# Own PSUM banks for a second block of tokens, block 0 first, one-word counts, and loop heads at the start of a fetch block

## The chip, the cores and the metric

The kernel runs on one core of one Trainium2 chip. The metric is the device time of one execution in microseconds (us). PE is the tensor engine, ACT the scalar engine, DVE the vector engine, POOL the GpSimd engine, SP the engine that issues the weight loads. Each engine has a sequencer that reads its instructions in order, waits on semaphores, takes branches, and hands the work on.

## The reference

One layer of a decoder trunk for 512 tokens of 1024 channels, float32. A token-mixing half (sliding-window attention and differential attention, merged by gates) comes first and isn't touched. The second half is a mixture of 32 experts, top 4 of 32 for each token:

```python
logits = ht @ w_router + b_router
top_val, top_idx = lax.top_k(logits, 4); top_w = softmax(top_val)
# token slots grouped by expert, each group padded to blocks of 128 rows
gu = xb @ w_gate_up[e] + b_gate_up[e]            # 1024 -> 2048
h  = clamped_swiglu(gu)                          # 1024
ys = (h @ w_down[e] + b_down[e]) * weight        # 1024 -> 1024, summed per token
```

The 2048 token slots fall on 32 experts, 64 on average. An expert with up to 128 tokens has one block of 128 rows, one with more has two to four. How many is known only at run time, from the router. With the inputs used here 35 blocks are worked on.

## The kernel before

**Weights.** An expert has 12 MB of weights, loaded in 12 halves of 1 MB (`gate_up_half`, 8, and `down_half`, 4) into eight slots `rawm`. A product has to be exact to more than one pass of fp32r gives, so each weight half w is split: ACT rounds it to `wh` (`split_high`, L1100, four buffers), DVE subtracts, `wl = w - wh` (`split_low`, L1178, in place). The activations are split in the same way. A half is then 4 x 3 products of 128 x 512 on PE: wh with high, wl with high, wh with low (`multiply`, L1009 to L1011). The first of two halves has a bias product in front (`biased`, L1015).

**An expert.** `xy[b]` holds the gathered rows of block b. PE transposes them, 8 times 128 x 128, into PSUM banks 5 and 6 (`tokens_transposed`, L987); ACT copies the rounded part to `xh` (L1107), DVE the rest to `xl` (L1185). Eight gate and up halves follow. Gate sums are read by ACT (L1117), up sums by DVE (L1208, L1212). The activations `actv` are transposed into banks 5 and 6 too (`act_transposed`, L1001), and copied to `ah` (ACT, L1125) and `al` (DVE, L1193). Four down halves follow, whose sums ACT copies to `xy` (`outputs`, L1140), and POOL scatters them to the rows `y_d` (`scatter`, L1286 and L1289). For the expert two later POOL gathers new rows into the same `xy` (`gather`, L1267 and L1270).

**Order.** `passes` writes out the order. Body e does: the eight gate and up halves of expert e, the token transposes of e + 1, the four down halves of e - 1, the activation transposes of e. Bodies 1 to 30 stand in a hardware loop of 15 passes with two bodies each, one such loop on each of PE, ACT, DVE and SP (POOL has its own); body 0 and body 31 stand outside. Each loop starts with a branch prefetch hint for its closing branch (`hint_back_edge=True`).

**Further blocks.** Code for blocks 1 to 3 stands in front of that for block 0 in every step, under `If(more >= b)` (`Expert.further`, L893). For an expert with one block PE branches over it (L894). On PE this skipped code is three quarters of the loop. `Expert.__init__` reads one word per expert from the table `nk` (L866): 4 times the number of further blocks of all earlier experts, plus the expert's own number. It is taken apart with `// NB` and `% NB`.

**Banks.** Block 0 sums gate in bank 0 and up in bank 1 (down: 0 and 1). Block b > 0 sums both in bank 1 + b, one after the other: `ps[:, 1 + b if b else up, :]`. So up has to wait until gate was read, and one output half for the other. All transposes use banks 5 and 6: the transposes of a second block wait until the first ones were copied by ACT and DVE, and block 1 goes before block 0.

**On ACT and DVE** the copies of the transposed activations of expert e (`act_high`, `act_low`) stand in body e + 1: those of further blocks at its start, those of block 0 behind its first `split`.

## Time and profile before

| | us |
|---|---|
| median of 3 runs (1966.46 to 1977.33) | 1967.62 |
| the profiled execution | 1976.37 |
| its span, first to last instruction | 1974.6 |
| PE busy | 1702.7 |
| DVE busy | 1315.6 |
| ACT busy | 1028.1 |
| POOL busy | 250.7 |
| mean granted clock of PE | 0.925 |

The span has three parts: up to about 500 us the token-mixing half and the router, from there to about 1917 us the experts, then the weighted sum of the experts' rows. Matmul durations overlap in the records: a product of 128 x 512 is shown with 0.39 us and the next starts 0.23 us after it. So starts are compared, and idle time, not the sum of durations. The clock is shown as a share of 2.4 GHz; 0.50 is 1.2 GHz. A row with `q` behind the engine's name is one of its sequencer.

### The profile page before, as it was taken

The page shows a single profiled execution, that of the slowest core. Times are in us where ns is not written, and L with a number is a line of the kernel's source. Part 1 is how long each engine was busy: PE and PEld are TensorE (multiplying, and loading weights), DVE is VectorE, ACT ScalarE, POOL GpSimd, SP SyncE. Part 2 cuts the span into 40 slices and gives each one's busy share as a digit, 9 for nine tenths or more (in the row PEclk, how much of TensorE's full clock was granted, in tenths as well). Part 3 has the DMA queues.
Part 4 walks back from the last instruction along what each step waited for, and adds up shares of the span by engine and source line. Part 5 has one row for each costly group of instructions (what it writes and reads, how often), then busy time and mean ns, then how long its engine had stood idle before and what let it go on. Part 6 is the DMA issues. An engine that isn't in the chain of part 4 may idle for free.

```text
span 1974.6 us, 24769 instructions
## 1 busy us (share of the span) xinstructions
PE 1702.7 (86%) x7526; PEld 1314.8 (67%) x7527; DVE 1315.6 (67%) x1024; ACT 1028.1 (52%) x922; POOL 250.7 (13%) x232
## 2 busy tenths in 40 slices
PE   6999976695389998899999999898999998989860
PEld 1688854443368777777777877776777786767650
DVE  0454468734378887466888888855688888456645
ACT  2323234421357776355777777644567776445530
POOL 2000000112201111001111111110111111101110
PEclk8899986787589999999999999998999999989985
DMA  7575430011689998566999999955799999567835
GB/s 228 199 243 204 149 120 1 25 57 53 227 292 362 351 364 300 203 246 245 344 357 354 361 345 362 359 207 207 251 353 355 355 358 340 197 213 254 300 138 220
DMA packets 245566, 498.54 MB, mean 252 GB/s; under 512 B 16811, under 2 KB 17927, under 8 KB 244737
## 3 DMA queue, kind: packets, MB, share of 16 engines
q1 hardware_dynamic: 228288, 458.26, 64.9%
q0 software_dynamic: 14448, 34.72, 5.2%
q8 instruction: 201, 3.29, 0.7%
q10 hardware_dynamic: 2610, 2.11, 0.3%
q14 instruction: 19, 0.16, 0.0%
HBM read 490.22 MB, written 27.09 MB: 262 GB/s over the span
## 4 chain that ended last, share of the span: by engine, by line
PE 66%; issue 4%; DMA 4%; DVE 3%; ACT 2%; POOL 1%; DVEq 1%; ACTq 0%; POOLq 0%
PE ps L1009 19%; PE ps L1011 19%; PE ps L1010 19%; PE ps L621 3%; PE ps L1015 3%; PE ps L987 2%; DMA xy<-h_ffn,icur 1%; PE ps L1001 1%; DMA expert_rows<-xy,icur 1%; DMA x1e<-x_after_mixing 1%; ACT wh L1100 1%; POOL icur L1286 1%; PE ps L641 0%; DVE wl L1178 0%; DVE yo L1343 0%
## 5 line engine op out<-in xcount | busy, mean ns | idle before, releaser
L1178 DVE TENSOR_TENSOR wl<-rawm,wh 128x2048 fp32r<-128x2048 f32 x384 | 876.1, 2290 | 323.6 <-ACT wh L1100 318.0
L1100 ACT ACTIVATE wh<-rawm 128x2048 fp32r<-128x2048 f32 x384 | 736.2, 1918 | 484.0 <-PE ps L1011 480.3
L1009 PE MATMUL ps<-wh,xh 128*128 128x512 f32 x1120 | 473.6, 423 | 1.4 <-issue 1.1
L1011 PE MATMUL ps<-wh,xl 128*128 128x512 f32 x1120 | 442.5, 395 | 1.9 <-issue 1.7
L1010 PE MATMUL ps<-wl,xh 128*128 128x512 f32 x1120 | 442.9, 395 | 0.0
L1009 PEld LDWEIGHTS ps<-wh,xh 128*128 128x128 f32 x1120 | 216.2, 193 | 48.5 <-issue 8.2
L1011 PEld LDWEIGHTS ps<-wh,xl 128*128 128x128 f32 x1120 | 214.2, 191 | 47.0
L1010 PEld LDWEIGHTS ps<-wl,xh 128*128 128x128 f32 x1120 | 215.4, 192 | 44.4
L1009 PE MATMUL ps<-wh,ah 128*128 128x512 f32 x560 | 236.0, 421 | 0.0
L1010 PE MATMUL ps<-wl,ah 128*128 128x512 f32 x560 | 221.6, 396 | 0.0
L1011 PE MATMUL ps<-wh,al 128*128 128x512 f32 x560 | 221.4, 395 | 0.0
L1286 POOL COPY icur<-stab 128x1 int32 (+1 forms) x35 | 53.0, 1514 | 982.0 <-ACT xy L1140 982.0
L1011 PEld LDWEIGHTS ps<-wh,al 128*128 128x128 f32 x560 | 107.1, 191 | 23.3
L1010 PEld LDWEIGHTS ps<-wl,ah 128*128 128x128 f32 x560 | 107.4, 192 | 22.4
L1015 PE MATMUL ps<-bparts,sel 96*128 96x512 bf16 x210 | 84.1, 401 | 44.2 <-ACT actv L1117 14.9
L1009 PEld LDWEIGHTS ps<-wh,ah 128*128 128x128 f32 x560 | 108.3, 193 | 20.9
L1666 DVE TENSOR_TENSOR wlf<-raw,whf 128x2048 fp32r<-128x2048 f32 (+1 forms) x18 | 39.1, 2174 | 100.7 <-ACT whf L1442 100.7
L987 PE MATMUL ps<-ident,xy 128*128 128x128 f32 x280 | 40.1, 290 | 46.6 <-DMA xy<-h_ffn,icur 30.3
L1015 PEld LDWEIGHTS ps<-bparts,sel 96*128 (+1 forms) x210 | 20.6, 98 | 88.6 <-issue 57.6
L1270 POOL DMA_INDIRECT xy<-h_ffn,icur x35 | 67.5, 1930 | 31.8 <-POOL icur L1267 28.3
L1545 PE MATMUL ps<-whf,hh 128*128 128x512 f32 (+1 forms) x192 | 71.4, 372 | 0.0
L1547 PE MATMUL ps<-whf,hl 128*128 128x512 f32 (+1 forms) x192 | 71.1, 370 | 0.0
(224 smaller groups left out, 1692.4 us busy)
## 6 DMA issues: line engine op xcount, KB each, us to landing
rawm<-in_w_gate_up SPq DMA_DIRECT2D x256, 1024.0 KB, 6.5
rawm<-in_w_down SPq DMA_DIRECT2D x128, 1024.0 KB, 6.5
raw<-in_w_ada SPq DMA_DIRECT2D x24, 1024.0 KB, 10.0
raw<-in_w_in SPq DMA_DIRECT2D x16, 1024.0 KB, 5.4
yt<-expert_rows POOLq DMA_DIRECT2D x4, 2048.0 KB, 9.4
wo<-in_w_out SPq DMA_DIRECT2D x2, 2048.0 KB, 17.9
bias_vectors_repeated<-bias_vectors POOLq DMA_DIRECT2D x1, 2304.0 KB, 16.1
xs<-in_x ACTq DMA_DIRECT2D x1, 2048.0 KB, 25.4
```

The lines of the kernel that those rows point to most:

```text
L621: ins = nc.tensor.matmul(ps[:, 2 * b + half, :], src[:, k, t * P:(t + 1) * P], wo[:, 4 * b + k, half * UN:(half + 1) * UN], start=(k == 0) ...
L987: ins = nc.tensor.transpose(ps[:, 5 + k // 4, (k % 4) * P:(k % 4 + 1) * P], xy[b][:, k * P:(k + 1) * P], ident[:])
L1009: nc.tensor.matmul(dst, a_h[:, b, kk, :], wh[:, place.split(v), k, :], start=False, stop=False)
L1010: nc.tensor.matmul(dst, a_h[:, b, kk, :], wl[:, place.slot(v), k, :], start=False, stop=False)
L1011: ins = nc.tensor.matmul(dst, a_l[:, b, kk, :], wh[:, place.split(v), k, :], start=False, stop=kk == KC - 1)
L1015: nc.tensor.matmul(dst, sel[:, bass.ds(e, 1)].to_broadcast([96, P]), bias, start=True, stop=False)
L1100: nc.scalar.activation(flat(wh[:, place.split(v), :, :]), flat(rawm[:, place.slot(v), :, :]), ACT.Copy).then_inc(wh_done, 1)
L1178: nc.vector.tensor_tensor(flat(wl[:, place.slot(v), :, :]), flat(rawm[:, place.slot(v), :, :]), flat(wh[:, place.split(v), :, :]), ALU.sub ...
L1270: pool.indirect_dma_start(out=xy[b][:], out_offset=None, in_=h2_d, in_offset=bass.IndirectOffsetOnAxis(ap=icur[:, 0, b:b + 1], axis=0), bo ...
L1286: nc.gpsimd.tensor_copy(icur[:, 1, b:b + 1], stab[:, b, bass.ds(x.e + 1, 1)]).then_inc(scur[m], 1)
L1545: nc.tensor.matmul(dst, a_h, b_h, start=first, stop=False)
L1547: return nc.tensor.matmul(dst, a_l, b_h, start=False, stop=last)
```

## The change

Five edits go together.

1. **Banks.** A table `summed(b, n)` gives block 1 banks 2 (gate, first output half) and 7 (up, second output half); blocks 2 and 3 have one bank each, 3 and 4. `turned(b)` gives odd blocks banks 3 and 4 for their transposes, even ones 5 and 6.
2. **Order of blocks.** Both transposes and their copies on ACT and DVE do block 0 first, then the further ones (`first_then_further`). Since banks 3 and 4 belong to two uses, PE has new waits in the branches for further blocks, all on counts of earlier experts.
3. **act_high and act_low** as a whole move to the end of body e.
4. **Counts.** `nk` has two words per expert: the expert's own number, and the sum over earlier ones (`prefix`). The first is read in `__init__`; the second only in the branches for further blocks, once in each. The product that makes the table has 68 columns instead of 34.
5. **Heads.** The loops of PE, ACT, DVE and SP get `head_slot={eng.engine: 0}`: their first instruction is placed at the first place of a fetch block.

```diff
-    pick = NB * np.triu(np.ones((E, E + 2), np.float32), 2) + np.eye(E, E + 2, 1, dtype=np.float32)
+    pick = np.concatenate([np.eye(E, E + 2, 1, dtype=np.float32), np.triu(np.ones((E, E + 2), np.float32), 2)], 1)
...
-        nc.vector.tensor_copy(nk[:], ps[0:1, 5, 0:E + 2]).then_inc(nk_ready, 1)
+        nc.vector.tensor_copy(nk[:], ps[0:1, 5, 0:2 * (E + 2)]).then_inc(nk_ready, 1)
...
+    def turned(b):
+        return ps[:, 3:5, :] if b % 2 else ps[:, 5:7, :]
+    def summed(b, n):
+        return ps[:, ((0, 1), (2, 7), (3, 3), (4, 4))[b][n], :]
...
-            both = eng.value_load(nk[0:1, bass.ds(e + 1, 1)], min_val=0, max_val=NB * (T * TOPK // P) + NB - 1)
-            self.before = eng.snap(both // NB)
-            self.more = eng.snap(both % NB)
+            self.more = eng.value_load(nk[0:1, bass.ds(e + 1, 1)], min_val=0, max_val=NB - 1)
+        def prefix(self):
+            self.before = self.eng.value_load(nk[0:1, bass.ds(self.e + (E + 3), 1)], min_val=0, max_val=T * TOPK // P)
+            return self.before
...
+        def first_then_further(self, work, rest=None):
+            work(0)
+            self.further(work, rest)
+        def further(self, work, rest=None):
             with self.eng.If(self.more >= 1):
+                self.prefix()
                 work(1)
                 for b in range(2, NB):
                     with self.eng.If(self.more >= b):
                         work(b)
+                if rest is not None:
+                    rest()
...
-        with nc.Fori(0, E // 2 - 1, engines=[eng.engine], hint_back_edge=True) as k:
+        with nc.Fori(0, E // 2 - 1, engines=[eng.engine], hint_back_edge=True, head_slot={eng.engine: 0}) as k:
...
# tokens_transposed
             def work(b):
-                m = min(b, 1)
-                if b:
-                    pe.wait_ge(xg_in[1], (x.before + x.more) * 16)
-                    pe.wait_ge(xl_done[1], x.count(1, 0, b) - 1)
+                if b == 0:
+                    pe.wait_ge(xg_in[0], (e + 1) * 16)
                 else:
-                    pe.wait_ge(xg_in[0], (e + 1) * 16)
-                    pe.wait_ge(xl_done[1], x.all_more(1, 0))
+                    if b == 1 and not begins:
+                        acts = Expert(pe, e - 1).prefix() + START
+                        if not (isinstance(e, int) and e == 1):
+                            outputs = Expert(pe, e - 2).prefix() * U_D + START
+                        pe.wait_ge(al_done[1], acts)
+                        if not (isinstance(e, int) and e == 1):
+                            pe.wait_ge(y_copied[1], outputs)
+                        pe.wait_ge(g_ready[1], x.earlier(T_GU, 1))
+                        pe.wait_ge(u_ready[1], x.earlier(T_GU, 1))
+                    if b == 1:
+                        pe.wait_ge(xg_in[1], (x.before + x.more) * 16)
...
# act_transposed
+                if b == 1:
+                    tokens = x.before + x.more if last else Expert(pe, x.e + 2).prefix()
+                pe.wait_ge(act_ready[min(b, 1)], x.count(T_GU, 1, b))
+                if b == 1:
+                    pe.wait_ge(xl_done[1], tokens + START)
+                    pe.wait_ge(y_copied[1], x.before * U_D + START)
...
# gate_up_half_used
-                dst = ps[:, 1 + b if b else up, :]
+                dst = summed(b, up)
+                if v == 0 and b:
+                    outputs = Expert(pe, x.e - 1).prefix() * U_D + START if has_d else None
+                    pe.wait_ge(xl_done[1], x.all_more(1, 0))
+                    if has_d:
+                        pe.wait_ge(y_copied[1], outputs)
+                        pe.wait_ge(al_done[1], x.earlier(1, 1))
+                        pe.wait_ge(u_ready[1], x.earlier(T_GU, 1))
...
# down_half_used
-                    elif t:
+                    elif b > 1 and t:
                         pe.wait_ge(y_copied[1], x.count(U_D, 0, b))
...
# body of ACT; DVE's in the same way with act_low
-            if has_d:
-                act_high(before, before.further)
             for v in range(N_GU + N_D if has_d else N_GU):
                 split_high(place, v + SPL)
-                if v == 0 and has_d:
-                    act_high(before, at_once)
...
+            act_high(x)
```

## Rows read from the trace of the kernel before

**Rows 1.** The page, engines: busy us, share of the span, instructions.

```profile
PE 1702.7 (86%) x7526; PEld 1314.8 (67%) x7527; DVE 1315.6 (67%) x1024; ACT 1028.1 (52%) x922; POOL 250.7 (13%) x232
```

**Rows 2.** The page, chain of waits by line: share of the span.

```profile
PE ps L1009 19%; PE ps L1011 19%; PE ps L1010 19%; PE ps L621 3%; PE ps L1015 3%; PE ps L987 2%; DMA xy<-h_ffn,icur 1%; PE ps L1001 1%; DMA expert_rows<-xy,icur 1%; DMA x1e<-x_after_mixing 1%; ACT wh L1100 1%; POOL icur L1286 1%; PE ps L641 0%; DVE wl L1178 0%; DVE yo L1343 0%
```

**Rows 3.** Windows: us, busy of PE, PEld, DVE, ACT, POOL, clock, DMA share, GB/s.

```profile
1031.96:1067.88 35.92, 35.92 (x167) 29.14 (x166) 31.91 (x19) 26.68 (x18) 5.13 (x4) 1.00 1.00 365
1067.88:1105.00 37.12, 36.44 (x167) 29.02 (x166) 31.91 (x19) 26.79 (x18) 5.96 (x4) 1.00 0.98 351
```

**Rows 4.** Windows, three stretches with a second block, eight plain experts.

```profile
771.81:947.18 175.37, 154.86 (x675) 123.87 (x673) 105.44 (x64) 85.86 (x61) 18.53 (x14) 0.94 0.67 237
1275.20:1448.63 173.43, 152.36 (x674) 121.83 (x673) 105.40 (x64) 85.90 (x61) 19.08 (x14) 0.95 0.68 242
1667.89:1841.90 174.01, 151.74 (x674) 121.45 (x673) 105.37 (x64) 85.88 (x61) 18.80 (x14) 0.95 0.67 239
958.54:1251.55 293.01, 289.63 (x1330) 232.65 (x1329) 255.26 (x145) 213.86 (x144) 43.64 (x32) 1.00 0.99 357
```

**Rows 5.** Waits of PE (us, times, longest), then one row of its timeline.

```profile
PE ps L987 <- DMA xy<-h_ffn,icur: 30.3, 4, 21.8
PE ps L987 <- DVE xl L1185: 16.2, 3, 5.4
PE ps L1015 <- ACT actv L1117: 14.9, 6, 2.5
PE ps L1001 <- DVE al L1193: 13.9, 3, 4.7
PE ps L1015 <- ACT xy L1140: 7.5, 3, 2.5
...
778.25 1.97 PE L987 MATMUL ps<-ident,xy 128*128 128x128 f32 x8 [5.41 <-DVE xl L1185]
```

**Rows 6.** Windows, two stretches at the lower clock.

```profile
777.42:784.25 6.83, 6.00 (x18) 5.02 (x19) 2.00 (x2) 1.02 (x1) 0.00 (x0) 0.50 0.18 64
808.14:811.55 3.41, 3.24 (x8) 2.58 (x9) 1.95 (x1) 0.60 (x2) 0.00 (x0) 0.50 0.77 298
```

**Rows 7.** Line 1270, the gathers at 757.3 and 760.8, and their landing.

```profile
L1270 POOL DMA_INDIRECT xy<-h_ffn,icur x2: 1047/1644/2242, 757.3 to 760.8; - x2
DMA to landing us min/median/max: 8.8/8.8/8.8
```

**Rows 8.** Lines 866 and 925, 1134 to 1142: ns min/median/max, first and last start.

```profile
L866 PEldq TENSOR_LOAD <-nk x2: 308/308/308, 1140.0 to 1140.8; - x2
L925 PEldq COMPARE_BRANCH  x1: 960/960/960, 1138.8 to 1138.8; - x1
```

**Rows 9.** Timeline of PE at the same head.

```profile
1140.92 1.04 PE L1001 MATMUL ps<-ident,actv 128*128 128x128 f32 x8
1142.32 0.39 PE L1015 MATMUL ps<-bparts,sel 96*128 96x512 bf16 x1 [0.37 <-issue]
```

**Rows 10.** Timeline of ACT and of DVE behind a body's end.

```profile
1109.03 1.92 ACT L1100 ACTIVATE wh<-rawm 128x2048 fp32r<-128x2048 f32 x1 [1.43 <-PE ps L1011]
1110.86 1.01 ACT L1125 ACTIVATE ah<-ps 128x1024 fp32r<-128x1024 f32 x1
1110.98 2.29 DVE L1178 TENSOR_TENSOR wl<-rawm,wh 128x2048 fp32r<-128x2048 f32 x1 [1.54 <-ACT wh L1100]
```

**Rows 11.** DMA queues, 1066 to 1139.7: packets, MB, share of the time.

```profile
q8 instruction: 12, 0.20, 1.1%
```

**Rows 12.** Line 894, 1131.2 to 1134.9, and 1854 to 1860: ns and starts.

```profile
L894 PEldq COMPARE_BRANCH  x2: 225/294/364, 1131.3 to 1134.2; - x2
...
L894 PEldq COMPARE_BRANCH  x2: 236/2529/4822, 1854.5 to 1859.6; - x2
```

**Rows 13.** Timeline of PE at the loop's exit.

```profile
1859.50 0.58 PE L1015 MATMUL ps<-bparts,sel 96*128 96x512 bf16 x1 [3.58 <-issue]
...
1883.86 0.39 PE L1015 MATMUL ps<-bparts,sel 96*128 96x512 bf16 x1
```

More of the change, by code:

```diff
@@ L851, in program @@
     y_half_copied = [sem("y_half_copied0"), y_copied[0]]
[L853 removed]
+    passed = sem("passed")
     START = 1
@@ L1050, in work @@
             def work(b):
-                dst = ps[:, 1 + b if b else t, :]
-                if d == 0:
-                    pe.wait_ge(al_done[min(b, 1)], x.all_more(1, 0) if b else x.count(1, 0, 0))
+                dst = summed(b, t)
+                if d == 0 and b == 0:
+                    pe.wait_ge(al_done[0], x.count(1, 0, 0))
+                if d == 0 and b:
+                    gate_ups = x.before + x.more if after is None else x.before + x.more + after.more
+                    if b == 2:
+                        tokens = gate_ups if after is None or is_last(after.e) else Expert(pe, after.e + 2).prefix()
+                        pe.wait_ge(xl_done[1], tokens + START)
+                    pe.wait_ge(al_done[1], x.all_more(1, 0))
+                    pe.wait_ge(y_copied[1], x.earlier(U_D, 1))
+                    pe.wait_ge(u_ready[1], gate_ups * T_GU + START)
                 if h == 0:
@@ L1106, in work @@
                 act.wait_ge(xt_done[m], x.count(1, 0, b))
-                nc.scalar.activation(flat(xh[:, b, :, :]), flat(ps[:, 5:7, :]), ACT.Copy).then_inc(xh_done[m], 1)
-            x.blocks(work)
+                nc.scalar.activation(flat(xh[:, b, :, :]), flat(turned(b)), ACT.Copy).then_inc(xh_done[m], 1)
+            x.first_then_further(work)
         def gate(x, t, place, v):
@@ L1134, in work @@
                     if after is not None:
-                        act.wait_ge(xt_done[1], after.all_more(1, 0))
+                        act.wait_ge(xt_done[1], x.before + x.more + after.more + START)
                     act.wait_ge(y_out[1], x.stored(1))
@@ L1167, in body @@
                     outputs(before, v // 2 - 4, place, v, after)
+            act_high(x)
         passes(act, body)
         end = Expert(act, E - 1)
-        act_high(end, end.blocks)
         outputs(end, 0, LAST, 1, None)
@@ L1225, in body @@
             before = Expert(dve, e - 1) if has_d else None
-            if has_d:
-                act_low(before, before.further)
             for v in range(N_GU + N_D if has_d else N_GU):
@@ L1233, in body @@
                 split_low(place, v + SPL)
-                if v == 0 and has_d:
-                    act_low(before, at_once)
             if not has_d:
                 tokens_low(Expert(dve, e + 1))
+            act_low(x)
         passes(dve, body)
-        end = Expert(dve, E - 1)
-        act_low(end, end.blocks)
     def experts_pool(pool):
```

138 lines of the change are left out of this document (72 added, 66 removed).

## The prediction

> **What bounds the kernel now.** The page first. PE is busy 86% of the span, DVE and ACT 67% and 52% [rows 1]; in the chain that ended last the product lines (L1009 to L1011) alone hold 57% [rows 2]. So I read PE and ask when it doesn't run at its own pace. An expert in the middle of the loop is 144 products and 16 transposes, from 1031.96 to 1067.88: 35.92 us, PE busy throughout at clock 1.00 [rows 3]. Neither wait nor weight sets that length; its DMA share is 1.00 at 365 GB/s, so the loads have little room either. Three kinds of time are lost around it.
>
> First, the experts that have a second block: 35 gathers for 32 experts, so there are three, and one trip from their token transposes until the third expert after takes 175.37, 173.43 and 174.01 us [rows 4]. Its work is four periods of 35.92 (three experts, and the second block's 144 products) and 0.9 for the transposes at its end: 144.6. 89.1 us are lost over the three, with the clock at 0.94 and 0.95. The waits of PE [rows 5] name them: 16.2 and 13.9 us in front of the second transposes of tokens and activations (they need banks 5 and 6 back, by DVE xl and al), 14.9 in front of a bias product while gate and up share the block's one bank (ACT actv), 7.5 the same for the two output halves (ACT xy), 8.5 of the 30.3 on the gather (21.8 is the first expert's). Some of these are followed by stretches at the lower clock level, 1.2 GHz: 6.83 us of 0.50 after the 5.41 wait [rows 6].
>
> Second, the loop head. An expert that begins a pass takes 37.12 instead of 35.92 [rows 3]. Over the eight periods from 958.54 to 1251.55 (293.01 us [rows 4]), with four heads in them, it is 5.65 us over 8 x 35.92: 1.41 a head. I count 14 back edges; those after a slow stretch cost near nothing, in sum about 14.5 us.
>
> Third, what the change leaves: attention, routing, the first gather, the tail.
>
> **The change, part by part.** *Own banks.* A second block's gate and up get banks 2 and 7, so the 14.9 and the 7.5 go. Its transposes go to 3 and 4 and no longer wait for 5 and 6: the 16.2 and 13.9 go. With them goes most of the slow clock. What is late next? ACT and DVE have twice the time per half there, so not they. Scatter and gather stay: the gather that lets the third expert after begin is issued by POOL behind two scatters and the second's landing, none of which moves. Its 8.5 us stay, bounds 0 and 9.
>
> *What the new code adds.* A prefix is now read apart, and `Expert(pe, e - 1).prefix()` reads both words. One read is 0.78 us from one load to the next [rows 8]. In front of the second block's token transposes stand five reads, 3.9 us, and a few waits on counts that were reached an expert ago, 0.6. PE's queue covers about 3.2: PE's sequencer has issued the activation transposes when the closing branch starts, at 1138.8, and they end at 1141.96 [rows 8, 9]. That leaves a gap of 1.3 to 1.6 and perhaps 0.8 of slow clock, 3 x 2.4 = 7.2; at the first gate half three reads more, 0.8 for the expert that starts mid-pass. Bounds: 0 if all is covered, 3 x 4.5 + 3.4 = 17 if nothing is.
> Of the 89.1, 8.5 (gather), 1.5 (the head in the third stretch), 8.0 (reads) and 1 for ends stay: **-70**, bounds -80 and -55.
>
> *First transposes lead.* PE does block 0 first. The gathers still go second block first; block 0's, issued at 760.8, landed 8.8 us later for transposes at 771.81 [rows 4, 7]: 2 us of room, so nothing.
>
> *act_high and act_low move to the end of the body.* On ACT it will follow the last output copy, before the next weight rounding. Idle ahead of that is 1.43 us, and ah takes 1.01; on DVE the idle is 1.54 and al takes some 1.22 [rows 10]. Both fit: nothing. Without the cover it would be 0.2 us a period at a queue four halves deep, still nothing on PE. DVE's `rest` and ACT's waits concern the three experts alone.
>
> *One-word counts.* At a head PE's sequencer reads two experts, divides and takes remainders; now one read and no arithmetic, -0.9 us, of which at most the visible 0.4 to 0.5 gap counts. In the others it is under the queue. POOL's chain gets 0.8 shorter at best. The wider count product and copy, once, are below 0.1.
>
> *Aligned heads.* Here the sign is decided. PE's loop body is 2878 instructions (counted in the compiled program of before), of 64 B. In the 73 us of a pass 12 instruction packets of 0.20 MB in all arrive [rows 11]: 16 KB, 256 instructions each, so the body is fetched anew in every pass. Where in a block does it lie? The branches over a further block take 222 to 250 ns, but some 340 to 464: those that jump into another block (one of each in rows 12). They fit one placing only: head at place 114, closing branch at place 175 of the twelfth block. And the branch that enters that block, at 1134.2, takes 364 ns [rows 12]; the closing branch, issued at 1138.8, is through 960 ns later [rows 8], 5.5 us after the entry. The other passes show the same 5.3 to 5.5; where PE was slow it takes only 353. So the loop's first block is asked for when the last is entered, and is there some 5.4 us later. Where a block wasn't asked for at all, at the loop's exit, the branch stands 4822 ns, and PE has a gap of 3.58 us and slower products behind it [rows 12, 13].
> The change makes the body longer: 14 skipped prefix reads per expert at 4 instructions each (56), and on balance 21 more for reads and waits in the first gate half, 18 for tokens, 16 for the first output half, 10 for activations, less 2: 119, and 117 for the pass's other expert, 3114 in all. With the head at place 0 the closing branch is at place 41 of a thirteenth block (29 to 53 with my counting error). And the activation transposes now come first, with some 70 skipped instructions between them and the branch. So the last block is entered by that skip, and the closing branch is reached at once: it will stand 5 us in every pass instead of 0.7 to 1.5. From the skip: 5.4 to the head, 1.65 to the first product (2.55 now, from 1139.8, 0.2 ahead of the first read, to 1142.32, less one read and the arithmetic [rows 8, 9]), less 3.2 of queue: PE idle 3.9, where it is 0.4 to 0.5 now. The nearest row is the exit: idle 3.58, then 24.4 for 96 products that take 22.75 at full clock (1.6 of slow clock) [rows 13]. I take 4.0 + 1.5 = 5.5 a head, bounds 0 (found in time) and 7.4 (the slow clock lasts 6.83 as after the 5.41 wait). The second stall, when the block after the head's is late too, goes, as a head at place 0 has a whole block to run on; it is inside the 1.41.
> 14 x 5.5 = 77, and 2.7 more at each of the two heads where a second block is due, less 14.5 now: **+68**. The exit now runs on within its block: 5.4 becomes 2, -3.5. Entry: one branch, +1. And behind a late head the gather of 8.5 is no longer late in two of three cases, -5.7. Heads in all: +60.
> ACT's body has 252 instructions, DVE's 253, and no instruction packets are theirs in the loop; 50 more leave that so: 0, bounds 0 and 30.
>
> The Trainium skill ("Runtime: NRT & Kernel Launch", Instruction fetch mechanics) has blocks of 16 KiB with 256 instructions, as the packets here show, and says that the next page is fetched while the current one runs, so that a crossing is "mostly hidden". By that rule heads cost nothing, and the sum is the first rival's. The rows speak for a fetch that is hidden only where 5.4 us of work are left in the block.
>
> **Sum.** -70 + 60 = -10, against the profiled execution, 1976.4 (span 1974.6 and 1.8 around it), which lies 8.8 above the median of 1967.6; I go by the median: **1957**.
>
> **Rivals.**
> *The closing branch finds its block.* My count is off by over 41, or the loop's first block is asked for earlier than I read. Then the 14.5 of the heads fall to about 1 instead: -70 - 13 + 1 = -82: 1886 (if the heads only stay as they are, 1898). For it: I have counted code that I haven't seen compiled. Against: 41 of 236 is much, and the 5.4 us recur in each pass.
> *The heads outweigh the banks.* One mechanism, the closing branch: 4.0 us idle and after it the long half-clock stretch, 3.4 lost, at every head. 14 x 7.4 + 5.4 - 14.5 - 3.5 + 1 - 5.7 = +86; less 70: +16, 1984. It decides from (70 + 5.7 + 14.5 + 2.5 - 5.4)/14 = 6.2 us a head. For it: 6.83 us at 0.50 after a 5.41 us wait; against: 3.41 us after a 2.49 one (808.14 on), and 1.6 lost after the 3.58 one [rows 5, 6, 13].
> *The banks don't do it.* PE waits for the reads instead and half of the 70 is lost: -35 + 60 = +25: 1992. Against: the reads are priced by their rows and small.
>
> **How the numbers follow.** Forecast 0.58 (its own range 1935 to 1977), block found in time 0.28, heads outweigh 0.11, banks fail 0.03. 0.5%, what a measurement of this kernel tells, is 10 us: within the forecast, at -10, 0.31 is faster, 0.24 same, 0.03 slower. With the 0.28 faster and 0.14 slower: 0.59, 0.24, 0.17. Range 1884 to 1984.
>
> **What would show it.** The closing branch (L925, PE's sequencer) at about 5000 ns in 14 passes, and a gap of 4 us in front of each odd expert's first bias product, followed by a clock of 0.50; 13 instruction packets a pass. Token and activation transposes of a second block without a wait on xl or al, no wait on actv or xy. The prediction is wrong if the closing branch stands below 1 us: then the time is near 1886.

## The result and the profile after

The changed kernel takes **1978.97 us** (median of 20 runs, 1971.69 to 1985.96), the kernel before beside it 1972.16 us (20 runs, 1964.47 to 1980.11): a ratio of 1.0035, 95% interval 1.0022 to 1.0047. It is slower by some 7 us, a third of a per cent; the forecast, 1957, lies 10 us under the kernel before by its own sum.

The page of the changed kernel, engines and the queue of instruction blocks (columns as in [rows 1] and [rows 11]):

```profile
span 1979.5 us, 24740 instructions
PE 1707.8 (86%) x7526; PEld 1321.7 (67%) x7527; DVE 1317.6 (67%) x1024; ACT 1030.1 (52%) x922; POOL 226.7 (11%) x232
q8 instruction: 217, 3.56, 0.7%
```

PE is busy for as long as before [rows 1]; 217 blocks of instructions arrive, where the kernel before had 201. The waits of PE, us in total, times, longest, to be held against [rows 5]:

```profile
PE ps L1057 <- issue: 54.0, 16, 6.4
PE ps L993 <- DMA xy<-h_ffn,icur: 27.0, 2, 21.7
PE ps L1057 <- DVE wl L1225: 21.4, 6, 5.6
PE ps L993 <- issue: 5.8, 3, 2.6
```

The 52.5 us on DVE xl, DVE al, ACT actv and ACT xy in the three stretches are gone. In their place stand 54.0 us in front of bias products (L1057), for which no releaser is found: the instruction came late. 49.5 us of them stand at ten of the 14 loop heads. Of the six put down to DVE wl four lie at heads too (3.65, 3.93, 3.84, 3.60 us): at the second of them wl was written by 1070.4 and the sequencer past its first skip by 1070.6, so there the two end almost together, and run 4 below, where neither is left, tells which of them leads. The next rows say by what: the closing branch (L943) over the whole run, then around one head the skip over the activation transposes of further blocks (L909) and the closing branch (ns min/median/max, first and last start), and the gap that PE shows there:

```profile
L943 PEldq COMPARE_BRANCH  x16: 89/4819/5876, 557.0 to 1862.2; - x16
...
L909 PEldq COMPARE_BRANCH  x1: 995/995/995, 1142.1 to 1142.1; - x1
L943 PEldq COMPARE_BRANCH  x1: 5739/5739/5739, 1143.3 to 1143.3; - x1
...
1144.39 1.04 PE L993 MATMUL ps<-ident,actv 128*128 128x128 f32 x8
1150.73 0.60 PE L1057 MATMUL ps<-bparts,sel 96*128 96x512 bf16 x1 [5.30 <-issue]
```

The skip enters the last block at 1143.1, the closing branch is through at 1149.0: 5.9 us. The instruction packets (queue q8) have times of their own. The head's block starts to move at 1146.5 here; at another head the last block was entered at 909.8 and the packet starts at 911.1, where the DMA engines were less busy. The q8 row of the windows 1146.50:1146.62 and 911.04:911.14, the closing branch of that second head, and both fetches as windows (columns as in [rows 3]):

```profile
q8 instruction: 1, 0.02, 56.3%
q8 instruction: 1, 0.02, 67.1%
L943 PEldq COMPARE_BRANCH  x1: 3547/3547/3547, 910.0 to 910.0; - x1
909.81:913.52 3.71, 2.92 (x17) 2.27 (x16) 0.88 (x1) 1.63 (x1) 0.00 (x0) 1.00 0.41 137
1143.13:1149.03 5.90, 2.30 (x15) 1.77 (x13) 4.78 (x3) 3.97 (x4) 1.50 (x1) 0.91 1.01 373
```

At all 14 heads the packet takes 0.9 to 1.1 us and the closing branch is through 1.36 to 1.54 us after its end. So the branch stands for this block and for nothing else; what differs is the time from the entry of the last block to the packet's start, 1.3 to 3.6 us (6.0 where the last block was entered early).

Windows of the changed kernel (columns as in [rows 3]): a head's expert, a plain one, another head's, the half-clock stretch behind its gap, one whole pass, and the three stretches of [rows 4]:

```profile
1065.95:1108.47 42.52, 38.59 (x167) 30.88 (x166) 31.99 (x19) 26.78 (x18) 3.74 (x4) 0.92 0.86 308
1108.47:1144.39 35.92, 35.92 (x167) 29.14 (x166) 31.99 (x19) 26.80 (x18) 5.59 (x4) 1.00 1.01 359
1144.39:1187.67 43.28, 37.98 (x168) 30.44 (x167) 32.01 (x19) 26.77 (x18) 3.74 (x4) 0.92 0.84 301
1147.94:1154.77 6.83, 4.04 (x10) 3.18 (x11) 2.03 (x2) 0.00 (x0) 2.63 (x4) 0.50 0.33 122
1065.95:1144.39 78.44, 74.51 (x333) 60.03 (x332) 63.98 (x37) 53.58 (x36) 9.33 (x8) 0.96 0.93 331
777.91:940.54 162.63, 150.25 (x674) 120.40 (x673) 102.33 (x61) 84.91 (x61) 16.19 (x14) 0.96 0.72 250
1288.80:1451.73 162.93, 151.02 (x674) 120.93 (x673) 102.34 (x61) 84.89 (x61) 16.39 (x14) 0.96 0.72 252
1687.79:1850.76 162.97, 148.71 (x674) 119.41 (x673) 106.74 (x64) 86.11 (x61) 18.54 (x14) 0.97 0.72 256
```

A head costs 42.52 - 35.92 = 6.6 and 43.28 - 35.92 = 7.4 us here, where it was 1.2 [rows 3]. The three stretches fell from 522.8 to 488.5 us. That gain and those heads cancel.

### The profile page after: what moved, and what is told of

It reads as the page before. It is cut to its first block, busy times and chain, and to the rows that moved or that the text cites. A ratio compares the mean times of both kernels' runs of the same rounds, so it can differ in the third digit from the quotient of the medians.

```text
span 1979.5 us, 24740 instructions
## 1 busy us (share of the span) xinstructions
PE 1707.8 (86%) x7526; PEld 1321.7 (67%) x7527; DVE 1317.6 (67%) x1024; ACT 1030.1 (52%) x922; POOL 226.7 (11%) x232
## 4 chain that ended last, share of the span: by engine, by line
PE 68%; DVE 4%; issue 4%; DMA 2%; ACT 2%; POOL 1%; POOLq 0%; ACTq 0%; DVEq 0%
PE ps L1051 20%; PE ps L1053 19%; PE ps L1052 19%; PE ps L621 3%; PE ps L1057 3%; PE ps L993 2%; DVE wl L1225 2%; ACT wh L1154 2%; DMA x1e<-x_after_mixing 1%; DMA xy<-h_ffn,icur 1%; DMA expert_rows<-xy,icur 1%; PE ps L641 0%; DVE yo L1388 0%; PE ps L634 0%; ACT h2t L692 0%
## 5 line engine op out<-in xcount | busy, mean ns | idle before, releaser
L1051 PE MATMUL ps<-wh,xh 128*128 128x512 f32 x1120 | 479.3, 428 | 0.0
L1052 PE MATMUL ps<-wl,xh 128*128 128x512 f32 x1120 | 448.0, 400 | 0.0
L1053 PE MATMUL ps<-wh,xl 128*128 128x512 f32 x1120 | 447.6, 400 | 0.2 <-issue 0.2
L1057 PE MATMUL ps<-bparts,sel 96*128 96x512 bf16 x210 | 84.9, 404 | 80.1 <-issue 54.0
L1057 PEld LDWEIGHTS ps<-bparts,sel 96*128 (+1 forms) x210 | 20.5, 98 | 124.4 <-issue 119.4
L1591 PE MATMUL ps<-wlf,hh 128*128 128x512 f32 (+1 forms) x192 | 71.0, 370 | 0.0
## 6 DMA issues: line engine op xcount, KB each, us to landing
bias_vectors_repeated<-bias_vectors POOLq DMA_DIRECT2D x1, 2304.0 KB, 15.7
```

The lines of the kernel that those rows point to most:

```text
L1051: nc.tensor.matmul(dst, a_h[:, b, kk, :], wh[:, place.split(v), k, :], start=False, stop=False)
L1052: nc.tensor.matmul(dst, a_h[:, b, kk, :], wl[:, place.slot(v), k, :], start=False, stop=False)
L1053: ins = nc.tensor.matmul(dst, a_l[:, b, kk, :], wh[:, place.split(v), k, :], start=False, stop=kk == KC - 1)
L1057: nc.tensor.matmul(dst, sel[:, bass.ds(e, 1)].to_broadcast([96, P]), bias, start=True, stop=False)
L1591: nc.tensor.matmul(dst, a_h, b_l, start=False, stop=False)
```

## The experiments

**Theory A**, the prediction's own: PE's closing branch stands until the head's block of 256 instructions is there, 5.4 us from the moment the last block was entered. **Rival B**: the new code itself (reads, waits, a longer body) costs the time, wherever the head lies. The first four runs move the head without touching the work, or the work without the head.

**1. The changed kernel, PE's head at place 110**

```diff
-        with nc.Fori(..., hint_back_edge=True, head_slot={eng.engine: 0}) as k:
+        with nc.Fori(..., hint_back_edge=True,
+                     head_slot={eng.engine: 110 if eng.engine == mybir.EngineType.PE else 0}) as k:
```

> The changed kernel with PE's loop head at place 110 of a block of 256 instructions instead of place 0 (other engines stay). The closing branch then lies at place 143 of the thirteenth block, and that block is entered by the skip behind the output halves, some 12 us of PE work ahead of the branch, as in the kernel before.
> Theory A (the head's block is asked for when the last block is entered, and is there 5.4 us later): the closing branch takes 0.3 to 1.5 us instead of 3.5 to 5.9, the gaps of 2.5 to 6.4 us in front of odd experts' bias products fall below 1 us, the half-clock stretches of 6.83 us behind them go, and the gain of the banks shows alone: 1972 - 70 = about 1902 (1890 to 1915).
> Rival B (the added reads, waits and the longer body cost the time, wherever the head lies): the closing branch still takes over 3 us or the gaps move elsewhere, and the time stays within 10 us of the changed kernel, 1970 to 1985.

Measured: 1951.87 us, ratio 0.9908 [0.9880, 0.9935]. Faster than the changed kernel, so the place counts, but above theory A's 1890 to 1915 and below rival B's 1970 to 1985: 50 us short of A's 1902. One end of a pass, two skips (L909) and the closing branch:

```profile
L909 PEldq COMPARE_BRANCH  x1: 4104/4104/4104, 1043.2 to 1043.2; - x1
L909 PEldq COMPARE_BRANCH  x1: 2787/2787/2787, 1049.2 to 1049.2; - x1
L943 PEldq COMPARE_BRANCH  x1: 3463/3463/3463, 1054.0 to 1054.0; - x1
```

These are three crossings into a new block, each of which stands. The first ends at 1047.3, the second at 1051.9 (4.7 us later), the third at 1057.5 (5.5 later). It isn't the closing branch alone: any crossing waits that comes too soon behind the one before.

**2. The changed kernel, heads not placed** (`head_slot` left away: head at about place 160)

> The changed kernel with no placing of the loop heads at all: PE's head falls at about place 160 of a block, and its closing branch at about place 193 of the thirteenth, with more than 5.4 us of work in that block.
> Theory A: the closing branch is short (0.3 to 1.5 us), but the first branch of the pass, which jumps over the second block's token transposes from instruction 6 to 120 of the body, now leaves the head's block at once. The next block has been asked for only when the head's was entered, so this branch stands 4 to 5 us instead: the same stall a branch later, and the time is about that of the changed kernel, 1965 to 1985.
> Rival B (only the closing branch's own jump back is dear, a crossing elsewhere is mostly hidden): both are short, time about 1900.
> Rival C (aligning the heads is what saves time): slower than the changed kernel by over 10 us.

Measured: 1963.46 us, 0.9959 [0.9941, 0.9977]. That is 1.5 us below theory A's range, and the stall moved as it has it, from the closing branch to the first skip:

```profile
L943 PEldq COMPARE_BRANCH  x1: 1164/1164/1164, 1053.0 to 1053.0; - x1
...
L909 PEldq COMPARE_BRANCH  x1: 4207/4207/4207, 1055.3 to 1055.3; - x1
```

Aligning the heads cost 15 us against leaving them alone, enough to turn a change of -0.4% into one of +0.35%. But it isn't what took most of the gain, as both layouts lose 6 to 7 us in each quiet pass.

**3. The kernel before, its heads at place 0**

```diff
-        with nc.Fori(0, E // 2 - 1, engines=[eng.engine], hint_back_edge=True) as k:
+        with nc.Fori(0, E // 2 - 1, engines=[eng.engine], hint_back_edge=True, head_slot={eng.engine: 0}) as k:
```

> The kernel before with nothing changed but its loop heads, which are aligned to blocks. PE's body of 2878 instructions then ends at place 61 of the twelfth block, entered by the skip behind the activation transposes of its further blocks; block 0's 16 transposes and a wait stand between that and the branch.
> Theory A: the closing branch takes 3.5 to 5 us in each of 14 passes, PE idles 3 to 5 us in front of the next bias product with half clock behind it, 50 to 75 us in all: 2020 to 2045. The difference between this kernel and the changed one is then the gain of the banks by itself, -50 to -70.
> Rival B (the new code costs the time, not the place of the head): within 10 us of the kernel before, 1962 to 1982.

Measured: 2008.78 us, 1.0191 [1.0164, 1.0217], below the 2020 to 2045 of theory A; closing branch 3882 ns in the median. Rival B falls: with not one instruction of the new code, the aligned head alone costs 38 us. The changed kernel is 30 us faster than this one: less than the -50 to -70 expected for the banks, and its own heads lose more (6.6 to 7.4 us a quiet pass against 3.5 to 6.0 here).

**4. The changed kernel, trimmed by 48 instructions**

```diff
-                self.prefix()
+                if prefix:
+                    self.prefix()
...
-            x.blocks(work)
+            x.blocks(work, prefix=h == 0)     # gate and up halves, output halves
```

The prefix isn't used where it is left away. PE's body is 3058 instructions, the closing branch at place 241 of the twelfth block.

> The changed kernel with its heads aligned as they are, but without the read of the prefix in the second gate, up and output half (h = 1), where nothing uses it. That takes 48 instructions out of PE's body: 3058, so that the closing branch falls at place 241 of the twelfth block, which is entered by a skip behind an output half, over 5.4 us of work ahead; 12 blocks a pass instead of 13.
> Theory A: no stall at the closing branch (0.3 to 0.5 us) and none behind the head, whose block is whole: both stalls of a head are gone, and the time is 1972 - 70 - 13 = about 1889 (1878 to 1905). Instruction packets: 12 a pass.
> Rival B (a head at place 0 itself is dear, or the new waits are): the closing branch stays over 3 us, time 1965 to 1985.

Measured: 1914.45 us, 0.9726 [0.9698, 0.9755]. The line of the closing branch, one pass, and the three stretches:

```profile
L944 PEldq COMPARE_BRANCH  x16: 89/452/1144, 555.3 to 1786.4; - x16
...
1038.74:1110.59 71.85, 71.85 (x334) 58.29 (x333) 64.00 (x37) 53.55 (x36) 10.84 (x8) 1.00 1.01 361
760.62:918.33 157.71, 147.81 (x674) 118.80 (x673) 106.72 (x64) 86.10 (x61) 22.60 (x14) 0.98 0.75 267
1242.00:1399.88 157.88, 147.96 (x674) 118.95 (x673) 106.64 (x64) 86.10 (x61) 22.34 (x14) 0.97 0.77 271
1615.69:1776.36 160.67, 149.21 (x675) 119.77 (x673) 106.73 (x64) 86.09 (x61) 20.65 (x14) 0.97 0.75 263
...
PE ps L994 <- DMA xy<-h_ffn,icur: 37.7, 4, 22.0
PE ps L994 <- issue: 7.5, 3, 2.7
...
L909 PEldq COMPARE_BRANCH  x27: 222/227/2845, 1039.2 to 1108.3; - x27
```

Both stalls of a head are gone: the pass is 71.85 us with PE busy in all of it, twice the plain expert's 35.92 [rows 3]. The last row, the skips of the same pass, shows that blocks still come late: five of the 27 skips stand 2.0 to 2.8 us. Each time PE has enough in its queue, and loses nothing. That it is 1914 and not 1878 to 1905 is the stretches' doing: they hold 476.3 us, only 46.6 under [rows 4]: the waits on a gather behind the first expert's are 37.7 - 22.0 = 15.7 us, where they were 8.5 [rows 5].

**A new theory D** was tried next: the number of blocks is what bounds a pass (12 or 13, some 5.95 us each).

**5. The changed kernel without the hint** (`hint_back_edge=True` left away)

> The changed kernel without the hint that names the closing branch to the instruction fetch (hint_back_edge is left away; the heads stay aligned, same instructions otherwise but for the hint itself).
> Theory A (in the changed kernel the closing branch is reached right after the last block is entered, and the hint can only start the fetch of the head's block at that entry): without it the fetch starts at the branch itself, so the branch stands 4.8 us and more instead of 3.5 to 5.9; the pass gets 0 to 1 us longer and the time is 1975 to 1995. At the exit the next block is then the one that was asked for.
> Rival B (the hint is what makes the branch dear, for instance since it displaces the fetch of the next block): the branch is shorter than now by over 1 us, 1960 or less.
> Rival C (the hint still saves much): slower by over 20 us, 2000 or more.

Measured: 2002.92 us, 1.0141 [1.0102, 1.0180]; the branch 6248 ns in the median, up to 7556. That is rival C's (2000 or more, slower by over 20), and theory A misses by 8 us: the hint is worth 1.4 us a pass at the branch even though it comes late, and 24 us in all, where theory A had at most 1 us a pass. Without it 230 blocks arrive instead of 217 (`q8`), one more in most passes. At one closing branch, entered at 1154.8, two packets follow, at 1157.2 and 1158.3: first the block behind the last, in vain, then the head's.

**6. The kernel before, padded to 13 blocks**

```diff
                 for b in range(2, NB):
                     with self.eng.If(self.more >= b):
                         work(b)
+                        if b == 2 and self.eng.engine == mybir.EngineType.PE:
+                            for _ in range(3):
+                                self.eng.value_load(nk[0:1, bass.ds(self.e + 1, 1)], ...)
```

> The kernel before with its own banks, reads and waits, but with code added that never runs: three reads of a count inside each section for a third block (no expert here has one), on PE alone, 252 instructions a pass. PE's body is then 3130 instructions, its head at place 111 and its closing branch at place 168 of the thirteenth block, where the kernel before has 114 and 175 of the twelfth. Only the number of blocks that a pass runs through differs, 13 for 12.
> Theory D (new, from the runs so far: a block is asked for when the one before it is entered and is there 5.4 to 6.0 us later, so that a pass can't be shorter than its number of blocks by some 5.95 us: 71.4 for 12, 77.4 for 13; the passes without a second block took 71.8 us with 12 blocks and no stall at the head, 77 to 78.5 with 13 blocks wherever the head lay): quiet passes of 76.5 to 78.5 us instead of 73.0 to 73.5, branches over skipped sections that stand 1.5 to 4 us, and 14 x 3 to 5 us more: 2012 to 2045.
> Theory A alone (only the place of the closing branch counts): the closing branch stays at 0.7 to 1.5 us and the time within 10 us of the kernel before, 1962 to 1982.

Measured: 1972.19 us, 1.0009 [0.9986, 1.0032]. Theory D falls, 1972 for its 2012 to 2045: 252 instructions and one block more a pass, and nothing lost over the run. Passes of 72.6 and of 75.9 us stand side by side, so it is near an edge:

```profile
q8 instruction: 218, 3.57, 0.7%
...
1063.36:1135.92 72.56, 72.11 (x333) 58.16 (x332) 63.81 (x37) 53.45 (x36) 11.10 (x8) 1.00 1.00 357
1135.92:1211.83 75.91, 73.61 (x333) 59.41 (x332) 63.82 (x37) 53.36 (x36) 10.81 (x8) 0.98 0.96 347
```

**7. The trimmed kernel, PE's head at place 110**

> The run with 3058 instructions in PE's body (no read of the prefix in the second halves) with the head at place 110 instead of 0. The instructions that run are the same; the pass now runs through 13 blocks instead of 12, and the closing branch is at place 95 of the last.
> Theory D (number of blocks by 5.95 us): quiet passes of 76.5 to 78 us instead of 71.8, total 1914 + 14 x 3 to 5 = 1945 to 1985.
> Rival E (the 48 instructions fewer are what saved the time, by themselves): the time stays within 12 us of that run, 1902 to 1926.

Measured: 1967.68 us, 0.9960 [0.9932, 0.9987]; closing branch 4152 ns, quiet passes 76.9 to 78.7 us. Rival E falls: the 48 instructions fewer save nothing by themselves, what counts is where they put the edges. Theory D had the right number here for a wrong reason, as run 6 shows.

What is left, **theory T**: a block is asked for when the one before it is entered, and comes 4.7 to 6 us later (at two heads behind a second block's stretch 3.7); it costs what the block's own work, and the some 3 us that PE still has in its queue, don't cover. Not all of a block is work: a section of a further block is jumped over in 0.22 us and fills a third of one. I added up each layout's pass instruction by instruction (product 0.2365 us, transpose 0.1125, branch 0.24, load of a count 0.35, other register work 0.09, queue 3.2, and 5.4, 5.7 or 6.0 from a block's entry to the next). The sum is an estimate, and its single steps aren't printed here. The next three runs were chosen by that sum.

**8. The trimmed kernel, PE's head at place 16**

> The trimmed kernel (3058 instructions in PE's body) with the head at place 16 instead of 0. That moves every instruction of the loop by 16 places and changes none of them; the closing branch then lies at place 17 of the thirteenth block instead of place 241 of the twelfth, and that block is entered by the skip behind the activation transposes, 1 instruction or two before the branch.
> Theory T (a block is asked for when the block before it is entered and is there 5.4 to 6.0 us later; it costs where less work than that is left in a block, less the some 3 us that PE has in its queue; what counts is where the edges fall in the pass, not their number): closing branch 4 to 6 us, quiet passes of 76.5 to 79 us instead of 71.8 to 72.3, total 1914 + 14 x 4.5 to 7 = 1975 to 2010.
> Rival E (the 48 instructions fewer save the time by themselves): within 12 us of the trimmed kernel, 1902 to 1926.

Measured: 1983.69 us, 1.0065 [1.0042, 1.0089], as theory T has it. The closing branch lies at place 1 of the thirteenth block (241 + 16 = 257), not at 17 as expected; the skip still enters that block right in front of it. Sixteen places, no instruction changed, and 69 us lost against the trimmed kernel. Over the run, then a pass (against the 71.85 of run 4):

```profile
L944 PEldq COMPARE_BRANCH  x16: 89/5176/5937, 557.6 to 1866.2; - x16
...
1070.51:1149.25 78.74, 73.62 (x334) 59.40 (x333) 64.01 (x37) 53.56 (x36) 9.57 (x8) 0.98 0.93 332
```

**9. and 10. The kernel before, PE's head at places 128 and 208**

```diff
-        with nc.Fori(0, E // 2 - 1, engines=[eng.engine], hint_back_edge=True) as k:
+        with nc.Fori(0, E // 2 - 1, engines=[eng.engine], hint_back_edge=True,
+                     head_slot={eng.engine: 128} if eng.engine == mybir.EngineType.PE else None) as k:
```

> The kernel before with its loop head on PE at place 128 of a block instead of 114, nothing else. The last block is then entered by an earlier skip, and the block behind the head is left later.
> Theory T: adding up the pass instruction by instruction, with 5.4 to 6.0 us from entering a block to the next one and 3.2 us of queue, PE idles 0 to 0.9 us a pass instead of 1.2 to 2.7. Closing branch 0.3 to 0.7 us, quiet passes of 71.8 to 72.8 us instead of 73.0 to 73.5, total 1972 - 14 x 0.7 to 1.3 = 1954 to 1963.
> Rival H (the 1.4 us of a head in the kernel before is the branch and the reads themselves, not the fetch): within 4 us of the kernel before.

Measured: 1966.06 us, 0.9974 [0.9953, 0.9996]: 4 us less, not the 9 to 18 expected. The quiet passes kept 72.9 to 73.2 us; the sum is some 1 us a pass too kind to this place. By its time alone this run doesn't tell theory T from rival H. The trace shows where the stall went, to the second skip behind the head (3137 here, 2.3 to 3.4 us in the quiet passes):

```profile
L894 PEldq COMPARE_BRANCH  x2: 231/1684/3137, 1133.9 to 1137.3; - x2
```

The sum hangs on 3 us of queue that I took to be always there; that the queue was short at this skip is my reading, no run varied it.

> The kernel before with its loop head on PE at place 208, nothing else: the same 2878 instructions. The closing branch falls at place 13 of the thirteenth block, entered right ahead of it, and the first skip behind the head, from instruction 11 to 97, crosses into the next block at once, while that one has only been asked for on entering the head's.
> Theory T: two fetches stand one behind the other: closing branch 4.7 to 5.3 us and the first skip 3.6 to 4.2, PE idle 7.5 to 8.7 us a pass instead of 1.2 to 2.7 and slow clock behind it; quiet passes of 79.5 to 83 us, total 1972 + 14 x 6 to 10 = 2056 to 2112.
> Rival B (late code costs once per pass at most): 2020 to 2045, as with the head at place 0.
> Rival E (placing doesn't matter without the new code): within 10 us of the kernel before.

Measured: 2066.43 us, 1.0475 [1.0443, 1.0507], in the range of theory T and out of both rivals'. The closing branch (L925) over the run, PE's first skips (L894) behind one head, and that pass:

```profile
L925 PEldq COMPARE_BRANCH  x16: 88/4738/6177, 558.6 to 1946.9; - x16
L894 PEldq COMPARE_BRANCH  x2: 237/1562/2886, 1102.3 to 1105.8; - x2
...
1061.88:1143.41 81.53, 74.75 (x333) 60.20 (x332) 63.82 (x37) 53.43 (x36) 9.01 (x8) 0.94 0.91 321
```

Two fetches stand one behind the other: 4.7 us at the branch, 2.9 at the first skip. The same 2878 instructions take 100 us more than at place 128.

**11. The trimmed kernel, POOL scatters block 0 first**

```diff
-            x.blocks(work)
+            x.first_then_further(work)      # in scatter()
```

> The trimmed kernel (no read of the prefix in the second halves, head at place 0, 12 blocks a pass), and POOL scatters an expert's block 0 ahead of its second block. The gather that lets the third expert after begin waits for block 0's scatter to land; in the trimmed run that scatter was the second of two (issued at 897.32, landed 905.70, gather issued at 908.32, landed 916.37) and PE waited some 5.3 us for the gather at each of the three places, with 2 us of slow clock behind it.
> Theory F: block 0's scatter is issued first, some 4 us earlier, and the gather with it: the wait of PE on the gather falls from 5.3 to about 1 us or goes, with its slow clock: 3 x 4 to 7 us less, 1914 - 12 to 21 = 1893 to 1902.
> Rival G (the gather waits for the transfers' own rate, or for POOL's second scatter in front of it): within 4 us of the trimmed run, 1910 to 1918.

Measured: 1896.99 us, 0.9607 [0.9572, 0.9642]: 17 us less than run 4, within theory F's 1893 to 1902. Of the waits on the gather for the third expert after, 4.9, 5.5 and 5.4 us in run 4, one of 1.0 is left; two of 1.3 and 1.1 are new, ahead of an expert with a second block. Theory F holds.

**12. The same, and one-word reads of a prefix**

```diff
+    def prefix_of(eng, e):
+        return eng.value_load(nk[0:1, bass.ds(e + (E + 3), 1)], ...)
...
-                        acts = Expert(pe, e - 1).prefix() + START
+                        acts = prefix_of(pe, e - 1) + START
...
-                            outputs = Expert(pe, e - 2).prefix() * U_D + START
+                            outputs = prefix_of(pe, e - 2) * U_D + START
...
-                    tokens = x.before + x.more if last else Expert(pe, x.e + 2).prefix()
+                    tokens = x.before + x.more if last else prefix_of(pe, x.e + 2)
```

> The trimmed kernel with POOL's scatter of block 0 first, and with the reads of an earlier or later expert's prefix reduced to the one word that is used: in front of a second block's token transposes three reads instead of five, ahead of its activation transposes two instead of three. Each read took 0.64 to 0.78 us on PE's sequencer, and PE idled 2.1 us in front of the second token transposes with 3 us of slow clock behind.
> Theory R (the reads are what keeps PE waiting there): 1.3 to 1.5 us less idle before each of three token transposes, and the slow clock behind them gone, 3 x 1.5 to 4.5: 1897 - 5 to 13 = 1884 to 1892.
> Rival S (another wait ends last there): within 3 us of 1897.

Measured: **1889.12 us**, 0.9585 [0.9547, 0.9624], the fastest of all. The medians differ from run 11 by 8 us, the ratios by 4, and their intervals overlap; what decides is PE's idle time before the three second token transposes, 3.2, 3.3 and 3.4 us in run 11 and 1.9, 1.9 and 1.9 here, as theory R has it. The three stretches:

```profile
760.43:911.60 151.17, 146.96 (x675) 118.30 (x674) 102.39 (x61) 84.89 (x61) 16.59 (x14) 0.99 0.75 264
1235.81:1386.04 150.23, 145.36 (x675) 117.07 (x674) 102.46 (x61) 84.88 (x61) 18.66 (x14) 1.00 0.76 270
1601.50:1752.87 151.37, 147.03 (x674) 118.32 (x674) 101.71 (x61) 84.33 (x61) 19.55 (x14) 0.99 0.75 263
```

452.8 us: 70.0 less than [rows 4]. The figure forecast for the banks is there, but not by the forecast's parts: that one still had 8.5 us of gather and 8.0 of reads standing, and here the gather is earlier, the reads are fewer and no late head lies in the stretches.

**All layouts together.** "Sum" is PE's idle time a pass by the added-up pass, at 5.4 and at 6.0 us a block; "over" is what the quiet passes (no second block; those from about 1000 to 1260 us) took beyond 71.84, half clock included.

| run and kernel | PE instructions in the loop's body | head at | closing branch at | it takes, median ns | sum, us | over, us | time, us |
|---|---|---|---|---|---|---|---|
| 4 trimmed | 3058 | 0 | 241 of 12th | 452 | 0 | 0.0 | 1914 |
| 12 fewer reads | 3037 | 0 | 220 of 12th | 460 | 0 | 0.0 | 1889 |
| 9 before | 2878 | 128 | 189 of 12th | 781 | 0 to 0.9 | 1.0 to 1.4 | 1966 |
| before | 2878 | 114 | 175 of 12th | 744 | 1.2 to 2.7 | 1.2 to 1.6 | 1972 |
| 6 padded | 3130 | 111 | 168 of 13th | 980 | 1.2 to 5.7 | 0.7 to 4.1 | 1972 |
| 1 changed | 3106 | 110 | 143 of 13th | 1008 | 1.5 to 5.7 | 4.4 to 7.2 | 1952 |
| 3 before | 2878 | 0 | 61 of 12th | 3882 | 3.6 to 4.5 | 3.5 to 6.0 | 2009 |
| 7 trimmed | 3058 | 110 | 95 of 13th | 4152 | 3.8 to 6.2 | 5.1 to 6.9 | 1968 |
| changed | 3106 | 0 | 33 of 13th | 4819 | 3.8 to 5.7 | 6.6 to 7.4 | 1979 |
| 8 trimmed | 3058 | 16 | 1 of 13th | 5176 | 3.8 to 5.7 | 6.7 to 6.9 | 1984 |
| 2 changed | 3106 | 160 | 193 of 13th | 784 | 4.3 to 5.8 | 6.5 to 6.7 | 1963 |
| 10 before | 2878 | 208 | 13 of 13th | 4738 | 7.5 to 8.7 | 9.7 to 10.2 | 2066 |

The sum was made after runs 1 to 7; runs 8 to 10 are its test, and run 9 its miss. It leaves out the half clock, which I take to be most of what "over" has beyond it. The places are worked out from the head's place and the count.

## Why the prediction was wrong

The mechanism was right: the banks' waits went, and late heads took the gain back. The sign came out wrong since **three terms were mis-sized**, all to the good side. By the prediction's own steps, on the profiled executions (spans of 1974.6 and 1979.5). Its base was low too: 1967.6 from three runs, where twenty give 1972.16, so the same -10 would read 1962.

- *Own banks, -89.1 of waits.* Right: no wait on xl, al, actv or xy is left in the three stretches. No engine behind them became the bound.
- *What the new code adds, 8.0.* Too small. PE idles 2.0, 2.6 and 1.1 us before the second token transposes, 0.8 to 1.0 before the bias products behind them, 0.7 to 0.8 at the first gate half of the expert that starts in mid-pass, some 1.7 at a head in front of the second block's, and slow clock follows most of them: in all some 19, against 8 and the 1 for ends. The reads behind the tokens' were taken as covered by the queue; as I read it, the queue is still short from the first gap when they come. Run 12 makes three reads less in each of the three places and gets 8 us back. **+10.**
- *The gather is no longer late in two of three cases, and its 8.5 stay at most.* It was hidden at two places, but the third wait is 5.3 us with some 3 of slow products behind it, as much as the three cost before. So nothing of the -5.7 came. With the heads mended it gets worse, 15.7 us (run 4): the experts ahead of it got faster, POOL's chain didn't. **+6.**
- *Aligned heads, 14 x 5.5.* The step that failed most plainly in its bounds: my 1.5 us of slow clock behind the gap was taken from the exit [rows 13], where the gap was 3.58. The gaps are 2.5 to 6.4 us, 4.6 in the mean (sum of 14: 64.5; I had 4.0), and around ten of them the clock stands at 0.50 for 6.83 us, as [rows 6] showed around the 5.41 gap, around the other four for 3.41. The length doesn't follow the gap: one of 3.93 has the long stretch, one of 5.31 the short. By what the transposes and the first products of each head take beyond their own pace it is some 92 us over 14 heads, 6.6 a head (4.2 to 8.5, so past my upper bound of 7.4), where 77 + 5.4 were forecast. The rival "the heads outweigh the banks" decided from 6.2 us a head and gave 1984; it is what happened, though with smaller heads than its 7.4 and with the reads' and the gather's help, so that its 1984 comes so near is partly luck. **+9.**
- *Why 4.6 and not 4.0.* I started the 5.4 us at the skip; in five passes the last block itself wasn't there when the skip wanted it (995 to 1089 ns, 368 to 466 in eight others). The chain of late blocks begins before the head.
- *Exit, -3.5.* Right, and a little more: 89 ns for the branch, no gap where 3.58 stood; some -6 with its slow products. *ACT's and DVE's bodies, act_high and act_low, the wider count product*: nothing seen, as forecast. *First transposes lead*: the first ones waited for nothing.
- The count of PE's body was 3114; it is 3106, the closing branch at place 33 for the forecast 41. *"The closing branch finds its block"* at 0.28 was too much for that: its condition was a miscount by over 41. Its time, 1886, is that of run 12 within 3 us, but that run is had by 69 instructions less and a shorter chain on POOL.

-10 + 10 + 6 + 9 is +15, less 2 to 3 more at the exit and some 5 by which the two profiled executions differ ahead of the first expert's products (the first gather is issued at 517.4 before and 513.0 after), which no part of the change explains: +7, with +5 between the two spans and +7 between the medians.

A block that is crossed "mostly hidden", the rule of the Trainium skill ("Runtime: NRT & Kernel Launch", Instruction fetch mechanics) that the prediction weighed, is borne out for PE's time by the passes of run 4 (12 crossings, nothing lost, though the sequencer stood up to 2.8 us) and not by those of the changed kernel (6.6 to 7.4 us a pass). The same section warns that a taken branch out of the two pages at hand stalls for its fetch; the closing branch of run 5, which has no hint and takes 6248 ns, is that case. The first skip of run 2 stood 4.2 us though it only jumps into the next block.

**Still open.** Why a block takes 4.7 us from entry to entry at one place and 5.9 at another. In the changed kernel it is 3.7 at the two heads where the DMA engines are less than half busy (0.41 at the one shown), and 4.3 to 6.0 at the 11 where they are 0.98 busy and more, so the packet may wait behind the weight loads. But in run 3 two heads at 0.56 and 0.62 took 5.3 and 5.4 like the rest, and no run varied the loads: it isn't shown. Open too are why place 128 gave only 4 us, and what the banks alone are worth with both heads silent and the old reads, which wasn't run (runs 4 and 9 stand 52 us apart, with 1.0 to 1.4 us of head a pass in the latter).

## What to carry to other kernels

This loop's body of some 3000 instructions was streamed anew in every pass, one block ahead. For a body like it, count what work PE has between one block edge and the next, skipped code included: sixteen places can move an edge onto a branch and cost 70 us (runs 4 and 8), and the same edit can look good or bad by where it puts the edges. Judge a change of code inside such a loop only with the head placed for each version. And when a wait is taken away, look for the chain that runs beside it (here POOL's scatters and gather): it gets back part of the gain unless it is shortened as well.

## What the runs showed of the hardware that I had not expected

- The same 2878 instructions take 1966 us with the loop head at place 128 of a block and 2066 at place 208; 3058 take 1914 at place 0 and 1984 at place 16.
- Not only the closing branch stalls: a skip behind the head stood 4.2 us (run 2), a skip inside the output halves 4.1 (run 1).
- The hint for the back edge still saves 24 us when the last block is entered right in front of the closing branch (run 5), and 13 blocks more arrive without it.
- A branch that jumps over a section within its block takes mostly 215 to 237 ns, into a block that is there 420 to 470, and 338 to 372 when it is the first jump behind an edge that was crossed in line, without leaving the block. I had read the last kind as a crossing in [rows 12]. That these are the three kinds is inferred from where the edges lie.
- From the end of a block's packet to the end of the branch that waited for it are 1.36 to 1.54 us at all 14 heads of the changed kernel; the packet itself takes 0.9 to 1.1.
- 252 instructions that never run, and one block more a pass, cost nothing measurable where the edges fall well (run 6).
